# Two chunks of a unit of weights take turns, product by product, instead of one after the other

## The reference, cut to what matters

```python
for l in range(DEPTH):                                   # 2 layers
    mod = (cond @ w_ada[l] + b_ada[l])[:, None, :]       # six vectors of 2048
    h = rms_norm(x) * (1.0 + sc1) + sh1
    z = h @ w_in[l]                                      # 2048 x 4160
    ...                                                  # three groups of heads
    mix = jnp.concatenate([out_a, out_b, out_c], axis=-1) @ w_out[l]   # 2048 x 2048
    x = x + g1 * mix
    h = rms_norm(x) * (1.0 + sc2) + sh2
    x = x + g2 * conv_ffn(h, ffn_w_up[l], ffn_conv_w[l], ffn_conv_b[l], ffn_w_down[l])  # 2048 x 11264, 5632 x 2048
```

## Time and profile before

| | |
|---|---|
| median of 3 runs | 2454.56 us (2453.03 to 2458.52) |
| profiled execution, span | 2452.9 us |
| PE busy | 2364.7 us, 96% |
| DVE busy | 1845.9 us, 75% |
| ACT busy | 1144.4 us, 47% |
| products (MATMUL) | 15360 |
| mean granted clock of TensorE | 0.979 |

### The profile page before, as it was taken

The page is one execution under the profiler, slowest core; times in us unless marked ns, Lnnn a source line. Parts: engine busy times, 40 slices in busy tenths (PEclk is TensorE's granted clock), DMA queues, the critical chain, the costliest instruction groups (busy, mean ns, idle before and its releaser), DMA issues.

```text
span 2452.9 us, 38201 instructions
## 1 busy us (share of the span) xinstructions
PE 2364.7 (96%) x15360; PEld 2047.0 (83%) x15360; DVE 1845.9 (75%) x2555; ACT 1144.4 (47%) x1613; POOL 295.7 (12%) x433
## 2 busy tenths in 40 slices
PE   5889999989999999999999999998999999999999
PEld 2578988888888888888887888888888888888888
DVE  2447876869998889888887685666999667766775
ACT  2233654355453455445544355535545345544553
POOL 3321321220101000110030121001010000000000
PEclk8799999999999999999999999999999999999999
DMA  8998786878989888998886876555897566656664
GB/s 298 337 298 267 253 281 222 285 234 255 298 282 319 281 258 262 294 300 255 258 272 217 269 246 219 177 171 178 253 300 226 191 189 189 190 192 190 190 190 147
DMA packets 450512, 596.90 MB, mean 243 GB/s; under 512 B 24172, under 2 KB 397984, under 8 KB 450080
## 3 DMA queue, kind: packets, MB, share of 16 engines
q1 hardware_dynamic: 394640, 392.47, 50.3%
q0 software_dynamic: 55296, 201.35, 25.4%
q10 hardware_dynamic: 400, 0.65, 0.1%
HBM read 592.30 MB, written 2.10 MB: 242 GB/s over the span
## 4 chain that ended last, share of the span: by engine, by line
PE 80%; DVE 10%; issue 3%; DMA 3%; ACT 3%; POOL 0%; ACTq 0%; DVEq 0%
PE bank L1094 79%; DVE wlo L1667 3%; DMA ada<-in_w_ada_dram 3%; DVE acc L1661 2%; ACT whi L1420 1%; DVE T L1686 1%; DMA rows<-in_b_ada_dram 0%; DVE yg L1693 0%; DVE r L1735 0%; DVE T L1750 0%; ACT sc_s L1541 0%; DVE yv L1693 0%; ACT hx L1488 0%; DVE hx L1771 0%; PE bank L1389 0%
## 5 line engine op out<-in xcount | busy, mean ns | idle before, releaser
L1094 PE MATMUL bank<-hx,whi 128*128 128x512 f32 (+1 forms) x4480 | 1363.5, 364 | 5.4 <-ACT z L1420 2.8
L1667 DVE TENSOR_TENSOR wlo<-raw,whi 128x1024 fp32r<-128x1024 f32 (+2 forms) x774 | 907.9, 1178 | 455.4 <-ACT whi L1420 453.9
L1420 ACT ACTIVATE whi<-raw 128x1024 fp32r<-128x1024 f32 (+2 forms) x774 | 780.6, 1017 | 815.0 <-PE bank L1094 774.5
L1094 PE MATMUL bank<-hx,wlo 128*128 128x256 f32 x3840 | 1091.2, 284 | 28.8 <-DVE hx L1771 20.4
L1094 PEld LDWEIGHTS bank<-hx,whi 128*128 128x128 f32 x4480 | 805.4, 190 | 146.3 <-issue 10.6
L1094 PEld LDWEIGHTS bank<-hx,wlo 128*128 128x128 f32 x3840 | 733.9, 191 | 47.0 <-issue 21.7
L1094 PE MATMUL bank<-mx,whi 128*128 128x512 f32 (+1 forms) x2096 | 613.8, 357 | 0.5 <-DVE xT L1717 0.5
L1094 PE MATMUL bank<-mx,wlo 128*128 128x256 f32 x1728 | 488.3, 283 | 0.0
L1094 PEld LDWEIGHTS bank<-mx,whi 128*128 128x128 f32 x2096 | 371.9, 190 | 64.8 <-issue 8.6
L1063 POOL DMA_DIRECT2D ada<-in_w_ada_dram x384 | 236.5, 618 | 1482.9 <-DVE acc L1661 927.8
L1094 PEld LDWEIGHTS bank<-mx,wlo 128*128 128x128 f32 x1728 | 329.6, 191 | 1.8 <-issue 1.6
(11 more groups left out here) (163 smaller groups left out, 1263.1 us busy)
## 6 DMA issues: line engine op xcount, KB each, us to landing
ada<-in_w_ada_dram POOLq DMA_DIRECT2D x384, 512.0 KB, 5.8
raw<-in_ffn_w_up_dram SPq DMA_DIRECT2D x352, 512.0 KB, 4.6
raw<-in_ffn_w_down_dram SPq DMA_DIRECT2D x176, 512.0 KB, 4.4
raw<-in_w_in_dram SPq DMA_DIRECT2D x128, 512.0 KB, 5.1
raw<-in_w_out_dram SPq DMA_DIRECT2D x48, 512.0 KB, 4.3
raw<-in_w_out_dram SPq DMA_DIRECT2D x32, 256.0 KB, 4.2
raw<-in_mla_w_uq_dram SPq DMA_DIRECT2D x12, 384.0 KB, 5.0
raw<-in_mla_w_ukv_dram SPq DMA_DIRECT2D x6, 512.0 KB, 6.2
```

Of the source, the lines that this page charges most:

```text
L1094: return pe.matmul(out_, lhsT, rhs, start=start, stop=stop, skip_group_check=True)
L1420: return act.activation(out_, in_, ACT.Copy)
L1667: i_ = tt(dst, src, high.bitcast(F32), ALU.subtract)
```

## The change

For each k of a unit, the products of the two chunks now take turns. Both banks are taken ahead of the first product of a pair's first unit. For a two-product block the order is low weights of chunk 0, low weights of chunk 1, high weights of chunk 0, high weights of chunk 1; for three products in the same manner. The signal `filled` for the first chunk stands on the second to last product of the pair. Products, operands, weight loads and the plan are the same; `ukvmm`, `uqmm` and all other steps stay.

```diff
--- before.py
+++ after.py
@@ -1140,36 +1140,45 @@
                     o = (u % SPLITS) * UNIT
                     es = plan.unit_entries(u)
                     pe.wait_ge(lo_ready, u + 1)
-                    for c_, key in enumerate(es):
-                        b = take(key) if x_.first else bank[plan.bank[key]]
-                        for j in range(x_.kt):
-                            k = x_.k0 + j
-                            input_ready(x_, k)
-                            start, stop = x_.first and j == 0, x_.last and j == x_.kt - 1
-                            a = o + (j * P if x_.what == "kr" else j * 256 + c_ * P)
-                            wh, wl = whi[:, a:a + P], wlo[:, a:a + P]
-                            if x_.what == "kr":
-                                i_ = three(b[:, 0:S], wh, wl, hi(hx, k), lo(hx, k), start, stop)
-                            elif x_.what == "win" and x_.i in TOKEN_PAIRS:
-
-                                a, ca = o + j * 256, 2 * k * S + c_ * P
-                                mm(b[:, 0:S], hx[:, ca:ca + P], whi[:, a:a + S], start, False)
-                                mm(b[:, 0:S], hx[:, ca:ca + P], wlo[:, a:a + S], False, False)
-                                i_ = mm(b[:, 0:S], hx[:, ca + S:ca + S + P], whi[:, a:a + S], False, stop)
-                            elif x_.what == "win" and x_.i not in TWO_PAIRS:
-                                i_ = three(b[:, 0:S], wh, wl, hi(hx, k), lo(hx, k), start, stop)
-                            elif x_.what == "wout":
-                                i_ = three(b[:, 0:S], wh, wl, mixed(k)[:, 0:S], mixed(k)[:, S:2 * S], start, stop)
-                            elif x_.what == "down" and (x_.b, x_.i) == LAST_DOWN:
-                                i_ = three(b[:, 0:S], wh, wl, hi(mx, k), lo(mx, k), start, stop)
-                            elif x_.what in ("win", "up"):
-                                i_ = paired(b, wh, wl, both(hx, k), start, stop)
-                            else:
-                                i_ = paired(b, wh, wl, both(mx, k), start, stop)
-                        if c_ == len(es) - 1:
-                            i_.then_inc(unit_done, 1)
-                        elif x_.last:
-                            i_.then_inc(filled, 1)
+                    two = [take(key) if x_.first else bank[plan.bank[key]] for key in es]
+                    for j in range(x_.kt):
+                        k = x_.k0 + j
+                        input_ready(x_, k)
+                        start, stop = x_.first and j == 0, x_.last and j == x_.kt - 1
+                        if x_.what == "kr":
+                            a = o + j * P
+                            i_ = three(two[0][:, 0:S], whi[:, a:a + P], wlo[:, a:a + P], hi(hx, k), lo(hx, k), start, stop)
+                            continue
+                        a = o + j * 256
+                        wh = [whi[:, a + c_ * P:a + (c_ + 1) * P] for c_ in range(2)]
+                        wl = [wlo[:, a + c_ * P:a + (c_ + 1) * P] for c_ in range(2)]
+                        x2 = mixed(k) if x_.what == "wout" else both(mx if x_.what == "down" else hx, k)
+                        if x_.what == "win" and x_.i in TOKEN_PAIRS:
+
+                            ah = [x2[:, c_ * P:(c_ + 1) * P] for c_ in range(2)]
+                            al = [x2[:, S + c_ * P:S + (c_ + 1) * P] for c_ in range(2)]
+                            for c_ in range(2):
+                                mm(two[c_][:, 0:S], ah[c_], whi[:, a:a + S], start, False)
+                            for c_ in range(2):
+                                mm(two[c_][:, 0:S], ah[c_], wlo[:, a:a + S], False, False)
+                            first_ = mm(two[0][:, 0:S], al[0], whi[:, a:a + S], False, stop)
+                            i_ = mm(two[1][:, 0:S], al[1], whi[:, a:a + S], False, stop)
+                        elif x_.what == "wout" or (x_.what == "win" and x_.i not in TWO_PAIRS) or (
+                                x_.what == "down" and (x_.b, x_.i) == LAST_DOWN):
+                            for c_ in range(2):
+                                mm(two[c_][:, 0:S], wh[c_], x2[:, 0:S], start, False)
+                            for c_ in range(2):
+                                mm(two[c_][:, 0:S], wh[c_], x2[:, S:2 * S], False, False)
+                            first_ = mm(two[0][:, 0:S], wl[0], x2[:, 0:S], False, stop)
+                            i_ = mm(two[1][:, 0:S], wl[1], x2[:, 0:S], False, stop)
+                        else:
+                            for c_ in range(2):
+                                mm(two[c_][:, 0:S], wl[c_], x2[:, 0:S], start, False)
+                            first_ = mm(two[0][:, 0:2 * S], wh[0], x2, False, stop)
+                            i_ = mm(two[1][:, 0:2 * S], wh[1], x2, False, stop)
+                        if len(es) == 2 and stop:
+                            first_.then_inc(filled, 1)
+                    i_.then_inc(unit_done, 1)
                 elif kind == "ukvmm":
                     l, v, u = t[1:]
                     o = (u % SPLITS) * UNIT
```

## The result

| | before | after |
|---|---|---|
| median, same chip and rounds | 2453.8 us | 2471.88 us |
| ratio, 95% interval | | 1.0066 [1.0053, 1.0078] |
| the same, second measurement | 2453.82 us | 2472.14 us, 1.0069 [1.0057, 1.0082] |
| span of the profiled execution | 2452.9 us | 2470.0 us |

The forecast was slower, 2460 us, range 2446 to 2469. The sign was right; the size was off by a factor of three, and the time lies outside the range.

A forecast was written before the change was run, and what follows sets the result against it. TensorE, busy 96% of 2452.9 us, was taken as the bound, its product steps unchanged. Bank waits +9.2, tails +1.4 and inputs -5.0 make +5.6 us, added to the 2454.56 median: 2460 us, range 2446 to 2469.

The forecast's parts named there:

- The banks don't matter: Product-to-product steps: changes of bank in the earlier trace show no gap, to 10 ns, so alternating banks changes nothing.
- I take 0, since the fixed part fits both kinds of block: Two-product blocks: 0.107 us per 256 columns plus fixed 0.013 a product, so the new order of lengths costs 0.
- The bound from the 0.23 us seen before a 256-column product: Block pairs: if 512 after 512 also takes 0.23 us, 3.3 ns more, 2280 times, +7.5 us.
- rival 3: Feed-forward stretches: two 512-column products in a row cost more, +7.5 us, 2468 us; chance 0.12.
- above 2.79 rival 3: Sign in a feed-forward stretch: 16 products taking more than 2.79 us would show rival 3; 2.77 us as before, the forecast.
- The rule beside the rows: Product step by the skill's N/2.4 + 2.5 ns: 325 ns a block against the rows' 347, 100 us less over 4560 blocks.
- Rival 4: Clock: new waits or the alternation lower it to 0.98 over the 1180 us, +24 us, 2484 us; chance 0.04.
- Bank waits and tails, +10.6: Pair starts wait for banks at 17 places, mostly projections and first output sweep, +9.2 us; four tails end later, +1.4.
- Inputs, -5.0: Where PE chases inputs, at norm transitions and after late mixed heads, fewer blocks remain after the last input: -5.0 us.
- Rival 2: The bank waits are swallowed, 0 to 3 of 9.2 us left, and the gains stay: 2451 to 2454 us; chance 0.22.
- PE's busy time of 300 to 560 us unchanged: Sign for rival 2 in the projection stretch; the forecast instead expected PE idle times of 0.3 to 0.7 us at pair starts.
- The range: Whole kernel: 2446 to 2469 us, leaving out most of rival 1, all of rival 4 and the edge of rival 3.

The follow-up runs named there:

- e3: Kernel before, but in feed-forward two-product blocks each product adds to the other bank than the one ahead, lengths still 256, 512 by turns: 2454.79 us against 2456.49.
- e5: Kernel before, but in feed-forward two-product blocks a chunk's four low products run first, then its four high, in one bank: 2473.01 us against 2457.61.
- e2: Kernel before, but feed-forward two-product blocks run lengths 256, 256, 512, 512 in one bank, without alternating banks: 2463.35 us against 2456.49.
- e9: The changed kernel itself, measured again beside the kernel before on the same chip: 2472.14 us against 2453.82, ratio 1.0069.
- e7: Kernel before, but three-product units alone take turns product by product with both banks taken early: 2468.23 us against 2457.61.
- e11: Kernel before, but in the last unit of three-product pairs chunks alternate product by product, so the first closes late; banks asked for as before: 2461.19 us against 2453.82.
- e6: Kernel before, but chunks take turns block by block only in units that chase their inputs, lengths 256, 512 kept: 2452.79 us against 2457.61.

## Why the prediction was wrong, step by step

- **The banks don't matter: right.** It was read from the changes of bank in the earlier trace rows to 10 ns. In e3 every step from 256 to 512 columns and six of a unit's eight from 512 to 256 change the bank, and they take 117 and 230 ns, as before.
- **"I take 0, since the fixed part fits both kinds of block": this step failed.** A fixed 13 ns was fitted to two totals, three products of 256 columns (360 ns) and one pair of 256 and 512 (347). With two unknowns and two totals every fit is perfect. A product of 512 columns in a run of its like was in no row, and the change shows 233 ns for it (e5 234), not the 227 that the fit gives (2 x 107 + 13). The bound from the 0.23 us seen before a 256-column product was the right one, 3.3 ns a pair; it stood as rival 3 with a chance of 0.12. Of its 7.5 us some 5 to 7 came: +6.9 in e2 by the ratio, 5.8 at equal clock. Its own sign was set wrong: "above 2.79 rival 3", while 3.3 ns a pair make 2.787 us a unit, and the steps named for "right" (0.12, 0.12, 0.23, 0.23) are rival 3's.
- **The rule beside the rows.** The 100 us less by N/2.4 + 2.5 ns were a comparison with the wrong figure: the Trainium skill (TensorE: Matmul & The Clock Gate, Back-to-back issue gap) calls that the gap of an isolated product, and gives about 131 ns at 512 columns for a stream with a weight load for each. The rows agree with neither (230 to 234 ns), and nothing in the forecast hung on it.
- **The clock outside the long stretches: put at nothing, without a reason.** Rival 4 looked only at the 1180 us of the feed-forward part, where 1.00 stayed. Outside it, PE was busy at half clock for 97.7 us instead of 77.4 in the profiled execution, and in e9 some 6 of 16 us go with the clock. Why it was lower isn't shown.
- **Bank waits and tails, +10.6: right, a little high.** e7 gives 10.3, and 9.0 at equal clock. Place by place: 0.36 for 0.34, 0.62 for 0.6 to 0.7, 2.10 for 1.6. The mechanism stands, too: early asking alone costs 4, and a late close without it shows no wait of PE in the trace (e11, 1.7 at equal clock).
- **Inputs, -5.0: right.** e6 gives -4.7, and less of it was swallowed by VectorE than I had feared.
- **Rival 2 (waits swallowed): out**, since e7 keeps most of them. Its sign, PE's busy time of 300 to 560 us unchanged, did come (247.79 and 247.70 us), though the waits are there: in a window of fixed times a wait that goes elsewhere (1.2 us at about 340 us) and other products make up for them. It was no good sign.
- **The range** ended 3 us short. It held the forecast with rival 3's lengths (2468), but not with the clock on top.

## What to carry to other kernels

A longer step between products shows in no busy share. It shows in the count of products that a busy stretch begins, and, free of what a shifted window adds, in the start times of the same products in both traces. The same comparison shows each wait at its place. Before reordering products for one property (the bank), write down what else the new order changes (here the succession of lengths, when a bank is asked for, and when an accumulation closes), and price a succession that no row shows by its bound, not by a fit through as many points as unknowns. Interleaving pays where the engine chases its inputs and costs where accumulators are few; it can be put in the one place and left out of the other. Where microseconds are few, compare the mean clocks of the runs before a difference is called a wait: e11's 7 us were mostly that.

## What the runs showed of the hardware that was not expected

On a TensorE that never waits, at clock 1.00 (2.4 GHz), the step of a product depends on its neighbours' lengths: 256 and 512 columns by turns take 347 ns a pair, in twos 348.4, in fours 350.9, each product with its own weight load; the steps in the middle of a run of four are 120 and 234, together 354. The bank that they add to makes no difference (2.773 us for 16 products with one or with 14 changes of bank among them). Why lengths by turns save these 7 ns isn't shown by any run here.
